# A transformer block pair in float32: in latent attention's first part, norm rows one product later than their sums, the angle steps spread differently, and the first keys and values ahead of the query latent's sums

## What is computed

```python
def mla_mixer(h, cos, sin, w_in, q_norm, w_q_up, kv_norm, w_kv_up, q_head_norm, k_head_norm, w_out):
    lat = h @ w_in                                  # 1024 -> 768 (queries) + 256 (keys, values) + 64 (rotary key)
    cq, ckv, k_pe = jnp.split(lat, [Q_LORA, Q_LORA + KV_LORA], axis=-1)
    q = (rmsnorm_2(cq, q_norm) @ w_q_up).reshape(B, S, N_HEADS, QK_HEAD)
    kv = (rmsnorm_2(ckv, kv_norm) @ w_kv_up).reshape(B, S, N_HEADS, QK_NOPE + V_HEAD)
    k_nope, v = jnp.split(kv, [QK_NOPE], axis=-1)
    k = jnp.concatenate([k_nope, jnp.broadcast_to(k_pe[:, :, None, :], (B, S, N_HEADS, QK_ROPE))], axis=-1)
    q = rope_tail(rmsnorm_2(q, q_head_norm), cos, sin)
    k = rope_tail(rmsnorm_2(k, k_head_norm), cos, sin)
    o = causal_attention(q, k, v)
    return o.reshape(B, S, N_HEADS * V_HEAD) @ w_out
```

## Time and profile before

| | us |
|---|---|
| median of 3 runs (lowest to highest) | 2670.73 (2667.22 to 2673.47) |
| the profiled execution's own time | 2672.47 |
| its span | 2670.9 |
| PE busy in the span | 2583.0 (97%) |
| DVE, ACT, POOL busy | 1243.9, 935.0, 628.2 |
| mean granted PE clock | 0.979 |

### The profile page before, as it was taken

The page is one execution under the profiler, slowest core; times in us unless marked ns, Lnnn a source line. Parts: engine busy times, 40 slices in busy tenths (PEclk is TensorE's granted clock), DMA queues, the critical chain, the costliest instruction groups (busy, mean ns, idle before and its releaser), DMA issues.

```text
span 2670.9 us, 28997 instructions
## 1 busy us (share of the span) xinstructions
PE 2583.0 (97%) x11787; PEld 2110.2 (79%) x11787; DVE 1243.9 (47%) x1616; ACT 935.0 (35%) x1376; POOL 628.2 (24%) x471
## 2 busy tenths in 40 slices
PE   8888799999999999999999999999998999999999
PEld 6766677788887888888888888888877787788887
DVE  7896654655625333335333333333335555433322
ACT  4475433444423333224323222322223444322321
POOL 4663301322202222101222101222002322222200
PEclk9998999999999999999999999999998899999999
DMA  4211221232232222322233232332321111232232
GB/s 164 71 40 32 95 63 63 84 98 95 87 98 77 94 95 95 95 91 87 88 102 97 93 95 95 98 100 91 95 89 52 41 42 34 91 105 95 93 95 89
DMA packets 67061, 227.30 MB, mean 85 GB/s; under 512 B 7280, under 2 KB 8816, under 8 KB 66928
## 3 DMA queue, kind: packets, MB, share of 16 engines
q1 hardware_dynamic: 66928, 225.44, 26.5%
HBM read 223.31 MB, written 2.10 MB: 84 GB/s over the span
## 4 chain that ended last, share of the span: by engine, by line
PE 86%; DVE 9%; issue 2%; ACT 2%; POOL 1%; DMA 0%; SPq 0%; DVEq 0%; POOLq 0%; ACTq 0%
PE main L374 19%; PE main L375 19%; PE main L376 19%; PE score L374 6%; PE score L376 6%; PE score L375 6%; PE out L374 3%; PE out L376 3%; PE out L375 3%; DVE cv L581 2%; DVE wl L366 1%; DVE hxl L494 1%; DVE stat L924 1%; DVE pt L959 1%; DVE tmp L1266 1%
## 5 line engine op out<-in xcount | busy, mean ns | idle before, releaser
L366 DVE TENSOR_TENSOR wl<-raw,wh 128x1024 fp32r<-128x1024 f32 (+2 forms) x435 | 563.6, 1298 | 836.7 <-ACT wh L358 836.2
L358 ACT ACTIVATE wh<-raw 128x1024 fp32r<-128x1024 f32 (+2 forms) x435 | 441.1, 1017 | 632.9 <-PE main L376 523.7
L374 PE MATMUL main<-hxh,wh 128*128 128x512 f32 x1264 | 498.6, 394 | 26.9 <-DVE mv_l L1118 14.5
L375 PE MATMUL main<-hxl,wh 128*128 128x512 f32 x1264 | 494.3, 391 | 0.0
L376 PE MATMUL main<-hxh,wl 128*128 128x512 f32 x1264 | 494.0, 391 | 0.0
L374 PE MATMUL main<-hh,wh 128*128 128x512 f32 x880 | 347.7, 395 | 0.7 <-POOL hl L1507 0.5
L376 PE MATMUL main<-hh,wl 128*128 128x512 f32 x880 | 347.5, 395 | 0.0
L375 PE MATMUL main<-hl,wh 128*128 128x512 f32 x880 | 347.5, 395 | 0.0
L374 PEld LDWEIGHTS main<-hxh,wh 128*128 128x128 f32 x1264 | 238.7, 189 | 84.5 <-DVE mv_l L1118 14.9
L376 PEld LDWEIGHTS main<-hxh,wl 128*128 128x128 f32 x1264 | 238.7, 189 | 50.2
L375 PEld LDWEIGHTS main<-hxl,wh 128*128 128x128 f32 x1264 | 238.8, 189 | 48.5
(11 more groups left out here) (376 smaller groups left out, 3502.8 us busy)
## 6 DMA issues: line engine op xcount, KB each, us to landing
raw<-in_wts SPq DMA_DIRECT2D x371, 512.0 KB, 3.6
raw<-in_wts SPq DMA_DIRECT2D x52, 384.0 KB, 3.1
raw<-in_wts SPq DMA_DIRECT2D x12, 256.0 KB, 2.6
x<-in_xT SPq DMA_DIRECT2D x4, 512.0 KB, 8.0
out<-x SPq DMA_DIRECT2D x8, 256.0 KB, 3.9
memx<-in_memT SPq DMA_DIRECT2D x1, 1024.0 KB, 8.6
band<-in_pool SPq DMA_DIRECT2D x1, 768.0 KB, 4.5
rope<-in_rope SPq DMA_DIRECT2D x1, 512.0 KB, 6.3
```

The costliest lines, as they stand in the source:

```text
L358: e.activation(wh[i % NCONV][:, 0:n], raw[i % NRAW][:, 0:n], ACT.Copy).then_inc(*sig.up("weight_high", ("high", i)))
L366: e.tensor_tensor(wl[i % NCONV][:, 0:n], raw[i % NRAW][:, 0:n], f(wh[i % NCONV][:, 0:n]), ALU.subtract) \
L374: e.matmul(o, ah, bh, start=start, stop=False)
L375: e.matmul(o, ah, bl, start=False, stop=False)
```

## The change

Four things move. No instruction is added or taken away, and none changes its shape.

1. The rows of mla are spread after lat 2 and no longer before it, and those of kvlat after lat 4. Lat 3 now stands ahead of the sums of kvlat, and lat 4 behind them. In the same way `low` of lat 4's unit is put in ahead of the angles.
2. The nine products turn over five banks (main0 to main2, score3, score4).
3. DVE does four angle steps together while it waits for the rows of mla, and then three for each of lat 3, 4 and 5, so that the Sin activations stand behind lat 6 on ACT (they stood behind lat 7), and the last step (cosine) behind lat 6 on DVE. The normed key-value latent (`tmp` by L1847, `ckh`, `ckl`) comes after lat 4's `cql`.
4. On PE the rotation of the rotary key stands ahead of lat 8, and keys and values of head 0 stand between lat 8 and the sums of cq. On DVE the sine product of the rotary key stands ahead of the two roots `cq_r` and `cq_r2`.

```diff
@@ build
+        latent_banks = Ring(banks[0:5])
@@ latent_tensor
             for m in range(2):
-                _, old = mainb.take(("lat", m))
+                _, old = latent_banks.take(("lat", m))
                 e.wait_ge(*sig.at(old))
...
             square_sums(e, "mla", KC - 1)
+            latent_product(e, 2)
             spread_rows(e, "mla", ("root", "mla"))
-            b, old = mainb.take(("lat", 2))
-            e.wait_ge(*sig.at(old))
-            linear(e, U_LAT + 2, b[:, :], normed("mla"))
+            latent_product(e, 3)
             square_sums(e, "kvlat", 1)
+            latent_product(e, 4)
             spread_rows(e, "kvlat", ("root", "kvlat"))
...
-            for m in range(6):
-                b, old = mainb.take(("lat", 3 + m))
-                e.wait_ge(*sig.at(old))
-                linear(e, U_LAT + 3 + m, b[:, :], normed("mla"))
-            square_sums(e, "cq", 5)
+            for m in range(5, 8):
+                latent_product(e, m)
             b, old = mainb.take("kpe turn")
             e.wait_ge(*sig.at(old))
             e.wait_ge(*sig.at("kraw"))
             e.matmul(b[:, :], perm[:, 1, :], kraw[:, :], start=True, stop=True).then_inc(*sig.up("q_turned", "kpe turn"))
+            latent_product(e, 8)
+            prep_tensor(e, 0, 0)
+            square_sums(e, "cq", 5)
@@ latent_scalar
-            for i in range(1, 4):
+            for i in range(1, 5):
                 high(e, U_LAT + i)
...
-                if m == 4:
+                if m == 1:
+                    for i in range(2):
+                        e.wait_ge(*sig.at(("ckn", i)))
+                        e.activation(ckh[:, i, :], lat_turn.of(("ckn", i))[:, :], ACT.Copy).then_inc(...)
+                    e.wait_ge(*sig.at("kpe sums"))
+                    e.activation(kpes[:, :], turnb.of("kpe sums")[:, 0:8:2], ACT.Copy).then_inc(...)
+                if m == 3:
                     angle_scalar(e)
@@ latent_vector
-            for i in range(1, 4):
+            for i in range(1, 5):
                 low(e, U_LAT + i)
-            mean_square(e, "mla", 1.0 / D)
+                if i == 3:
+                    mean_square(e, "mla", 1.0 / D)
+            for k in range(4):
+                angle_vector(e, k)
             for m in range(2):
-                angle_vector(e, 2 * m)
-                angle_vector(e, 2 * m + 1)
                 e.wait_ge(*sig.at(("unit", U_LAT + m)))
...
+                if m == 3:
                     mean_square(e, "kvlat", 1.0 / NMEM)
+                if m == 4:
                     for i in range(2):
                         s4, old = lat_turn.take(("ckn", i))
...
-                    for k in (2 * m - 2, 2 * m - 1):
-                        if k < 13:
-                            angle_vector(e, k)
+                for k in range(3 * m - 5, 3 * m - 2):
+                    if k < 13:
+                        angle_vector(e, k)
+                if m == 6:
+                    cosine_vector(e)
             mean_square(e, "cq", 1.0 / 768)
             st = stats.of(("st", "cq"))
+            e.wait_ge(*sig.at("kpe turn"))
+            e.wait_ge(*sig.at("cs"))
+            e.tensor_tensor(kper[:, :], mainb.of("kpe turn")[:, :], cs[:, 1, :], ALU.mult).then_inc(...)
             e.wait_ge(*sig.at(("root", "cq")))
...
@@ heads_tensor
-            for step in range(8):
+            for step in range(1, 8):
                 prep_tensor(e, 0, step)
```

More of the change, by code:

```diff
@@ L1753, in angle_vector, with cosine_vector @@
                 e.tensor_scalar(ang[:, :], ang[:, :], 3.1415925, -3.1415925, ALU.min, ALU.max).then_inc(*sig.up("angle", ("angle", k)))
-                e.wait_ge(*sig.at("half sin"))
-                e.tensor_scalar(cs[:, 0, :], red[:, :], -2.0, 1.0, ALU.mult, ALU.add).then_inc(*sig.up("angle", "cs"))
+        def cosine_vector(e):
+            e.wait_ge(*sig.at("half sin"))
+            e.tensor_scalar(cs[:, 0, :], red[:, :], -2.0, 1.0, ALU.mult, ALU.add).then_inc(*sig.up("angle", "cs"))
         def angle_scalar(e):
@@ L1762, in angle_scalar, with latent_product @@
             e.activation(red[:, :], red[:, :], ACT.Square).then_inc(*sig.up("sin", "half sin"))
+        def latent_product(e, m):
+            b, old = latent_banks.take(("lat", m))
+            e.wait_ge(*sig.at(old))
+            linear(e, U_LAT + m, b[:, :], normed("mla"))
         def latent_tensor(e):
             for m in range(2):
-                _, old = mainb.take(("lat", m))
+                _, old = latent_banks.take(("lat", m))
                 e.wait_ge(*sig.at(old))
-            linear_pair(e, U_LAT, mainb.of(("lat", 0))[:, :], mainb.of(("lat", 1))[:, :], normed("mla"))
+            linear_pair(e, U_LAT, latent_banks.of(("lat", 0))[:, :], latent_banks.of(("lat", 1))[:, :], normed("mla"))
             square_sums(e, "mla", KC - 1)
+            latent_product(e, 2)
             spread_rows(e, "mla", ("root", "mla"))
-            b, old = mainb.take(("lat", 2))
-            e.wait_ge(*sig.at(old))
-            linear(e, U_LAT + 2, b[:, :], normed("mla"))
+            latent_product(e, 3)
             square_sums(e, "kvlat", 1)
+            latent_product(e, 4)
             spread_rows(e, "kvlat", ("root", "kvlat"))
@@ L1806, in latent_scalar @@
             e.activation(s[:, :], lat_turn.of(("latent", 2))[:, :], ACT.Square).then_inc(*sig.up("q_squared", "kpe sq"))
[L1807 to L1811, removed]
             for m in range(6):
@@ L1837, in latent_vector @@
                 e.wait_ge(*sig.at(("unit", U_LAT + m)))
-                e.tensor_tensor(s[:, :], mainb.of(("lat", m))[:, :], rs[:, :], ALU.mult) \
+                e.tensor_tensor(s[:, :], latent_banks.of(("lat", m))[:, :], rs[:, :], ALU.mult) \
                     .then_inc(*sig.up("lat_scaled", ("latent", m), ("free", ("lat", m)), *([("free", ("rs", "mla"))] if m == 8 else [])))
                 if m == 2:
+                    e.wait_ge(*sig.at(("latent", 2)))
+                    e.wait_ge(*sig.at("kpe sq"))
+                    e.tensor_scalar(kraw[:, :], s[:, :], col("kh_pe"), None, ALU.mult).then_inc(*sig.up("k_raw", "kraw", ("free", ("latent", 2))))
+                    continue
+                e.wait_ge(*sig.at(("cqh", m - 3)))
+                e.wait_ge(*sig.at(("sq", "cq", m - 3)))
+                e.scalar_tensor_tensor(cql[:, m - 3, :], s[:, :], col("q_lat", m - 3), f(cqh[:, m - 3, :]), ALU.mult, ALU.subtract) \
+                    .then_inc(*sig.up("lat_low", ("cq", m - 3), ("free", ("latent", m))))
+                if m == 3:
                     mean_square(e, "kvlat", 1.0 / NMEM)
+                if m == 4:
                     for i in range(2):
```

22 lines of the change are left out of this document (7 added, 15 removed).

## The result

The changed kernel takes 2658.39 us (median of 7 runs, 2654.86 to 2667.69) against 2670.73 before (seven runs here, 2667.22 to 2679.40, with the same median as the three above); the ratio is 0.9952, 95% interval 0.9933 to 0.9971. In a second comparison it was 0.9945 (0.9926 to 0.9965; 6 runs, median 2660.04, against 2672.39). So the medians are 12.3 and 12.4 us apart, and the ratios say 12.8 and 14.7; forecast were 14.1 and 2656.6.

What follows compares the result with a forecast made beforehand. PE was taken to bound the kernel, busy 97%. 69.06 - (51.0 work + 0.3 + 0.9 waits + 2.5 slow clock) = 14.4, less 0.3: 14.1 us saved, giving 2658.4, or 2656.6 against the median; 8-in-10 range 2652 to 2664.

Steps and rivals of the forecast that it cites:

- Work and accounting: First sum of mla to first query-latent product: 51.0 us of PE work at full clock, 18.1 of 69.06 to gain.
- Part 1, rows: Rows of mla and kvlat one product later: 3.3 us of waits and 4.8 us of slow-clock loss go.
- The rival in which the clock falls there: Clock falls at the moved sums of mla and kvlat: saving 9.8, about 2661 us; chance 0.11.
- Part 2, banks: Five banks for the latent products: worth nothing alone, but make the late rows possible; with three, lat 3 would wait.
- Part 3, DVE's queue: Angle steps moved ahead of the rows lighten DVE between lat 3 and lat 8; last square of lat 8 at 48.6 us.
- DVE still late: DVE losses between lat 4 and lat 8 appear before the sums of cq: 4 us, saving 10, 2660.7; chance 0.15.
- Part 4, keys in front: Keys and values before the sums of cq: wait 6.6 us becomes 0.3, new wait about 0.9 at the keys' sums.
- The slow clock at the sums of cq: One clock fall around the sums of cq and the keys' sums: loss 1.7 to 3.4 us, 2.5 taken.
- The keys' rows: Head 0, behind the piece: PE waits for POOL's root, up to 0.7 us given back, 0.3 counted.
- slower: Heads behind the piece meet more clock falls when started at another moment: 2676.6 us with 40 added; chance 0.04.
- no gain: Piece ends earlier but PE then waits in head 0; 10 us would have to be lost: 2667; chance 0.07.

Runs made afterwards that it cites:

- three banks: Changed kernel with the latent products in three banks again and the rotary key's rotation in the bank named out; ratio 0.9950 (0.9934 to 0.9965).
- the old angle steps: Changed kernel with angle steps two by two again and Sin back behind lat 7 on ACT; piece 57.76 us, ratio 0.9953 (0.9933 to 0.9973).
- the own bank: Changed kernel with the rotary key's rotation in the bank named out instead of main0; piece 52.71 us, ratio 0.9951 (0.9925 to 0.9977).
- the keys' sums early: Changed kernel, rotation in the bank named out, head 0's keys' sums and root ahead of those of cq; piece 51.74 us, ratio 0.9961 (0.9940 to 0.9982).
- the products between the sums: Changed kernel, rotation in the bank named out, head 0 reordered so a product stands between each pair of sums; piece 51.38 us, ratio 0.9958.
- the product between: Changed kernel, rotation in bank out, keys' sums then rotary queries' product ahead of sums of cq, values' low part before their mean square; median 2655.56 us, ratio 0.9945.

## Why the prediction was right

**Work and accounting.** PE's own work of 51.0 us plus waits nearly gives the piece: 53.57 - 0.22 - 0.86 = 52.5 in the first profile, and 52.9 in the second. Of the 1.5 and 1.9 us that are over, 1.1 and 1.6 are the slow clock (2.2 and 3.1 us of PE's time at half clock inside the piece). The rest, about 0.4, is work that was counted too low; the terms listed add up to 50.8 and not 51.0.

**Part 1, rows.** Right in both halves. No wait at the rows and no fall of the clock at the two moved sums, in all ten profiles of kernels with this order: the sums of kvlat start 13.2 us behind those of mla in nine of them (13.1 forecast), the same to 0.01 us, and 14.9 in the one with three banks, by its wait. The rival in which the clock falls there is out. The witness for it was a place elsewhere in the kernel before with the same pattern.

**Part 2, banks.** Costed at nothing, and said to make part 1 possible. That was too strong: with three banks, and the rotation in a bank of its own, lat 3 waits 1.48 us and the piece is 1.2 longer, but the rows come a product later all the same.

**Part 3, DVE's queue.** Right in the number, half wrong in the mechanism. The turn-by-turn count put the last square at 48.6 us; it let PE go on at 48.9. With the old angle steps it was 51.6. But the prediction laid the 6.6 us of before to DVE's load alone, 6.4 us a turn for PE's 5.44, and its count has no wait for Sin. In the kernel before DVE idled 1.88 us at the cosine and 0.30 us behind it, between lat 7 and lat 8. Part 3 gains 2.7 us: these two waits are 2.2, the two steps beside them 0.8, and the turns up to lat 7 take 0.3 more than with the old steps. The new spread counts in that it has the angle ready for Sin one product earlier. The count for the changed kernel came out because in the new order this wait is gone. The rival "DVE still late" was shown not to come, but by little: PE did wait 0.2 us. DVE in order of time, lat 4 to lat 6 (columns as in the earlier trace rows):

```profile
2017.02 1.80 DVE L1857 SCALAR_TENSOR_TENSOR cql<-tmp,colsb,cqh 128x512 fp32r<-128x512 f32 x1 [1.39 <-ACT sq L426]
2018.74 1.40 DVE L1867 SCALAR_TENSOR_TENSOR tmp<-lat,colsb,turn 128x512 f32<-128x512 f32 x2
2020.18 1.35 DVE L1871 TENSOR_TENSOR ckl<-tmp,ckh 128x512 fp32r<-128x512 f32 x2
...
2030.43 1.22 DVE L367 TENSOR_TENSOR wl<-raw,wh 128x1024 fp32r<-128x1024 f32 x1
```

`cql` is again 1.80 us beside POOL's add, which runs from 2016.99 to 2018.27. The key-value tiles behind it start at 2018.74, when the add is over, and pay nothing (0.70 each), as the count had it. `cql`, with two inputs in SBUF, is what met the add; that such an instruction contends with GpSimd is what the Trainium skill (GPSIMD Engine Reference, Key points) says, and the 1.80 us for 0.75 agree.

**Part 4, keys in front.** 6.6 us of wait became 0.22 (0.3 forecast), the new wait is 0.86 (0.9 forecast). Undone alone it costs 6.6 us. The 0.86 us wait itself is worth 53.8 - 52.71 = 1.1 us of the piece, by the run with the own bank.

**What was mis-sized.** Small terms, and the place of one of them. The slow clock at the sums of cq was put at 2.5 us, all of it inside the piece. The slow stretch holds 6.0 us of PE's time, a loss of 3.0, in either profile; 1.1 and 1.6 of that lie in the piece and the rest behind its end. The keys' rows did not wait at all where I gave back 0.3, since POOL's root was ready at 2051.79 and PE, slowed, came at 2053.83. The piece shrank by 15.7 (mean of three against mean of two), where the sum had 14.4 for it; at head 1's keys, with the whole slow stretch behind, the gain is 14.2, where the sum had 14.1. That this agrees to 0.1 us is in part luck: the kernel before varies by 2.4 us between its profiles at this mark. I had the reason for the fall wrong too, if not its place: I described it by sums and a wait together. In the changed kernel the clock is down from 2044.8 on, before the 0.86 us wait begins, and the runs without that wait have the fall all the same.

**What stays open.** Whole runs show 12.3 and 12.4 us between medians, the piece 15.7 and head 1's keys 14.2. The 1.9 us between 14.2 and 12.3 are within what the parts outside scatter (the pair's end by 9 us, the heads by 6), but two and three profiles don't prove that nothing is given back behind head 1's keys. The rival "slower" is out; "no gain" is out by the ratios.

## What to carry to other kernels

Put a full product between a norm's sums and their rows, and judge whether the clock will stand it by a place in the same trace that already has the order. A wait at the end of a chain of turns is not the price of its last step: count the slower engine's turns against the bound one's, and read that engine's own idle times too. Here a side chain (Sin) that it waited for in the middle of its turns cost more than the steps that it did there; moved one turn earlier it cost nothing. Read parts of a few microseconds by the length of their own stretch in several profiles, not by whole runs, and end the stretch behind the slow clock that the part leaves.

## What the runs showed of the hardware

The clock fell to 1.2 GHz with PE never idle. In the run with the keys' sums early, PE went from 4.0 us of keys and values (the values 128 columns wide) through 3.24 us of one-column sums (2038.31 to 2041.55) without a gap, and the matmuls were slow from 2040.3 on, 2.0 us into the sums. The kernel before has such a place too, in a mixer at its start, where 32 one-column passes stand between products 512 columns wide:

```profile
233.86 4.34 PE L1130 MATMUL turn<-ones,cv 128*128 128x1 f32 x32
```

```profile
233.90:236.50 2.60, 2.60 (x26) 2.60 (x24) 0.13 (x1) 1.06 (x1) 0.00 (x0) 1.00 0.57 165
236.60:238.00 1.40, 1.40 (x8) 1.40 (x9) 0.00 (x0) 0.00 (x0) 0.00 (x0) 0.50 0.08 29
```

The clock fell 2.7 us into them, with PE busy since 231.0; it fell within them in 13 of the 14 profiles, and in the one with the old angle steps they passed at full clock. The 1.7 us of a norm's sums between products 512 columns wide, with no wait beside them, never brought it down: that is 104 places in the 14 profiles. Where PE waited beside such sums, as at the rows of mla and kvlat before, it came down in many cases. Six kernels have the values ahead of sums and no wait above 0.9 us there (the change, in both profiles, the own bank, three banks, the products between the sums, the keys' sums early, and the product between), and in each the clock fell once at this place, with an idle wait or without.

The whole kernel's time goes with the clock. The shortest and the longest of 79 runs of the kernel before lie at 2661.6 and 2690.9 us, and their time and their mean granted clock correlate with -0.95, 1.9 us for each 0.001 of mean clock.
